# A hybrid decoder trunk on Trainium2: weight halves between the RWKV triangular products one place further ahead, the fourth gate chunk in two halves, one merge behind the masks

## What is computed

```python
z = x @ w_in[l]
z_s5, z_lx, z_ly, z_rw, z_gate = jnp.split(z, IN_SPLITS, axis=-1)
y_s5 = s5_branch(z_s5, ...)      # ends with (y @ glu_w1) * sigmoid(y @ glu_w2)
y_lru = rglru_branch(z_lx, z_ly, ...)
y_rw = rwkv7_branch(z_rw, ...)   # per token: state = state*w + (state@a) b^T + v k^T
gates = jax.nn.sigmoid(z_gate.reshape(bsz, seq, N_BRANCH, D_MODEL))
merged = gates[:, :, 0] * y_s5 + gates[:, :, 1] * y_lru + gates[:, :, 2] * y_rw
x = layer_norm(ALPHA * x + merged @ mix_w_out[l], ln2_g[l], ln2_b[l])
```

## Time and profile before

| | before |
|---|---|
| median of 3 runs | 1610.47 us (1610.46 to 1610.76) |
| the profiled execution | 1610.43 us, span 1608.4 us |
| TensorE matmul busy | 1576.7 us, 98% of the span |
| VectorE busy | 1254.2 us, 78% |
| ScalarE busy | 796.2 us, 50% |
| granted TensorE clock | full (0.998 on the mean) |

### The profile page before, as it was taken

One profiled execution on the slowest core, in us unless ns is written; L12 is line 12 of the kernel. 1 busy time (PEld: TensorE's weight loads), 2 busy tenths in 40 slices (PEclk: granted clock), 3 DMA queues, 4 the chain that ended last, 5 costly groups with the idle time before them and its releaser, 6 DMA issues. The chain is left out here.

```text
span 1608.4 us, 31364 instructions
## 1 busy us (share of the span) xinstructions
PE 1576.7 (98%) x13277; PEld 1417.2 (88%) x13277; DVE 1254.2 (78%) x1620; ACT 796.2 (50%) x1018; POOL 234.2 (15%) x167
## 2 busy tenths in 40 slices
PE   9999999999999999999999999999999999999997
PEld 8888889999989988888888888999999999888886
DVE  6799899798668858766688998998885678587666
ACT  4655453663454545444455555346543545454443
POOL 2024520000000302001110435100000003010101
PEclk9999999999999999999999999999999999999999
DMA  8765744433436545666776656554334465456663
GB/s 250 216 190 183 207 135 136 138 121 107 147 118 210 171 130 171 186 193 186 210 199 188 191 177 182 158 145 125 113 117 145 128 210 165 144 163 191 190 190 131
DMA packets 380915, 267.74 MB, mean 166 GB/s; under 512 B 21132, under 2 KB 361576, under 8 KB 380776
## 3 DMA queue, kind: packets, MB, share of 16 engines
q1 hardware_dynamic: 377548, 255.16, 53.4%
q10 hardware_dynamic: 3228, 10.58, 2.1%
HBM read 264.66 MB, written 1.05 MB: 165 GB/s over the span
## 5 line engine op out<-in xcount | busy, mean ns | idle before, releaser
L1812 DVE TENSOR_TENSOR ring_lo<-ring_raw,ring_hi 128x1024 fp32r<-128x1024 f32 x461 | 598.0, 1302 | 200.4 <-ACT ring_hi L1389 195.8
L1389 ACT ACTIVATE ring_hi<-ring_raw 128x1024 fp32r<-128x1024 f32 x472 | 497.8, 1057 | 459.8 <-PE bank L765 203.2
L762 PE MATMUL bank<-xT,ring_hi 128*128 128x512 f32 x1344 | 335.5, 391 | 0.0
L762 PEld LDWEIGHTS bank<-xT,ring_hi 128*128 128x128 f32 x1344 | 244.1, 189 | 45.5
L735 PE MATMUL bank<-xT,ring_hi 128*128 128x256 f32 x864 | 251.3, 291 | 4.1 <-DVE ring_lo L1812 3.6
L736 PE MATMUL bank<-xT,ring_hi 128*128 128x256 f32 x864 | 244.3, 283 | 0.0
L737 PE MATMUL bank<-xT,ring_lo 128*128 128x256 f32 x864 | 244.2, 283 | 0.0
L765 PEld LDWEIGHTS bank<-xT,ring_lo 128*128 128x128 f32 x1344 | 183.3, 190 | 13.2 <-DVE ring_lo L1812 0.2
L765 PE MATMUL bank<-xT,ring_lo 128*128 128x256 f32 x1344 | 187.5, 282 | 0.0
L735 PEld LDWEIGHTS bank<-xT,ring_hi 128*128 128x128 f32 x864 | 165.3, 191 | 10.4 <-issue 5.4
L736 PEld LDWEIGHTS bank<-xT,ring_hi 128*128 128x128 f32 x864 | 165.5, 192 | 0.6 <-issue 0.5
(11 more groups left out here) (349 smaller groups left out, 2533.3 us busy)
## 6 DMA issues: line engine op xcount, KB each, us to landing
ring_raw<-in_w_in_dram SPq DMA_DIRECT2D x100, 512.0 KB, 4.0
ring_raw<-in_ffn_wg_dram SPq DMA_DIRECT2D x88, 512.0 KB, 3.9
ring_raw<-in_ffn_wu_dram SPq DMA_DIRECT2D x88, 512.0 KB, 3.9
ring_raw<-in_ffn_wd_dram SPq DMA_DIRECT2D x88, 512.0 KB, 3.4
ring_raw<-in_xa_wkv_dram SPq DMA_DIRECT2D x32, 512.0 KB, 3.9
ring_raw<-in_s_glu_w_dram SPq DMA_DIRECT2D x16, 512.0 KB, 3.4
ring_raw<-in_mix_w_out_dram SPq DMA_DIRECT2D x16, 512.0 KB, 3.9
ring_raw<-in_xa_wq_dram SPq DMA_DIRECT2D x16, 512.0 KB, 4.2
```

The lines of the kernel that those rows point to most:

```text
L762: mm(both, hi[:, k, :], xT_both[:, :, k, :], start=(k == 0), stop=(k == ND - 1), skip_group_check=True)
L1389: return nc.scalar.activation(o, i, func, **kw)
L1812: st.mark(tt(lo_flat(n), raw_flat(n), hi_flat(i), ALU.subtract), s_lo["dve"])
```

## The change

On TensorE, the three pieces between the four sets of products stand one place earlier: w2 (1,0) ahead of N1 instead of behind it, w2 (1,1) ahead of N2, and the first half of gate (4) ahead of N3. The second half of gate (4) stays behind N3. On VectorE, the low half of w2 (1,1) stands ahead of the V masks, that of gate (4,0) ahead of the M masks, that of gate (4,1) ahead of M plus eye, and `merge(3)` stands behind V plus eye instead of ahead of the W masks. ScalarE, GpSimd and SyncE keep their order. Lines of VectorE are one higher after the change, and some two.

```diff
--- before.py
+++ after.py
@@ -1124,12 +1124,13 @@
                     r = slice(C * par, C * par + C)
                     return mm(o, BK[r, q // NC, q % NC, 0, :], AR[r, q // NC, q % NC, 0, :], start=True, stop=True)
 
+                half_chunk("w2", 1, 0, zu_r)
                 pe.wait_ge(*at(s_Ge, 6))
                 for q in range(0, NQ, 2):
                     for par, qp in ((0, 0), (1, 1), (0, 1), (1, 0)):
                         last = turned_product(par, q + qp, banks[4 + par][C * qp:C * qp + C, q // 2 * C:q // 2 * C + C])
                 last.then_inc(s_N, 1)
-                half_chunk("w2", 1, 0, zu_r)
+                half_chunk("w2", 1, 1, zu_r)
                 pe.wait_ge(*at(s_Ge, 8))
                 pe.wait_ge(*at(s_Nb, 2))
                 for q in range(NQ):
@@ -1138,7 +1139,7 @@
                                                                                  (q % 8) * C:(q % 8 + 1) * C])
                         if q == NQ - 1:
                             last.then_inc(s_N, 1)
-                half_chunk("w2", 1, 1, zu_r)
+                half_chunk("gate", 4, 0, xT)
                 pe.wait_ge(*at(s_Nb, 4))
                 for q in range(NQ):
                     for par in range(2):
@@ -1147,7 +1148,7 @@
                                   AR[r, q // NC, q % NC, 0, :], BK[r, q // NC, q % NC, 0, :], start=True, stop=True)
                         if q == NQ - 1:
                             last.then_inc(s_N, 1)
-                gate(4)
+                half_chunk("gate", 4, 1, xT)
 
                 fill = [("gate", 5, xT), ("gate", 6, xT), ("gate", 7, xT), ("lru", 0, ly_r), ("lru", 1, ly_r)]
                 ORDER = ((0, 0), (1, 1), (0, 1), (1, 0))
@@ -2322,6 +2323,7 @@
                 st.then(stt(th_, h_, 1.0, th_, ALU.add, ALU.mult), s_lq)
                 masked_G(2)
                 masked_G(3)
+                lo_to("w2", 1, further=False)
 
                 def lru(t):
                     st.then(v.tensor_tensor_scan(h_[:, t, :], a_[:, t, :], gi_[:, t, :], 0.0, ALU.mult, ALU.add))
@@ -2337,16 +2339,14 @@
                 for par in range(2):
                     st.mark(tt(V_[:, par], bank(4 + par, 8, C),
                                const("off1T").unsqueeze(1).to_broadcast([P, NQ // 2, C]), ALU.mult), s_Nb)
-                lo_to("w2", 1, further=False)
                 merge(2)
+                lo_to("gate", 4, 0, further=False)
                 for par in range(2):
                     dve.wait_ge(*at(s_N, 2 + par))
                     st.mark(tt(M_[C * par:C * par + C], *masked("strictT", par), ALU.mult), s_Nb)
-                lo_to("gate", 4, 0, further=False)
+                lo_to("gate", 4, further=False)
                 dve.wait_ge(*at(s_Nb, 4))
                 st.mark(tt(M_, M_, eye, ALU.add), s_Me)
-                lo_to("gate", 4, further=False)
-                merge(3)
                 for par in range(2):
                     dve.wait_ge(*at(s_N, 4 + par))
                     st.mark(tt(W_[C * par:C * par + C], *masked("off1", par), ALU.mult), s_Nb)
@@ -2355,6 +2355,7 @@
                 lo_to("gate", 5, 0, further=False)
                 V16 = V_.rearrange("p a k c -> p (a k) c")
                 st.then(tt(V16, V16, eye, ALU.add), s_Vi)
+                merge(3)
                 dve.wait_ge(*at(s_lm, 1))
                 st.then(tt(gi_, gi_, th_, ALU.mult))
```

## The result

The median went from 1610.47 to **1617.44 us** (five executions each, 1616.65 to 1618.66 after). The ratio is 1.0042, with a 95% interval of 1.0032 to 1.0053. The forecast was slower, 1614.3 us, so the direction came as predicted, but 3.84 us were forecast and 7.0 came, and the time lies outside the range of 1612.7 to 1615.3. Further down, one execution of run 5 (1709.28 us at a mean clock of 0.849) and one of run 9 (7006.98 us) stand far from all others, and the ratios leave them out.

A forecast was written before the change was run, and what follows sets the result against it. TensorE, 98% busy at full clock, was taken as the bound; W products 1.92 us later in each of two layers gave 3.84 us on 1610.43, so 1614.3 us. The 8-in-10 range was 1612.7 to 1615.3.

The forecast's parts named there:

- What bounds the kernel: Whole kernel: TensorE is busy 98% of the span at full clock, so only its few gaps can pay.
- TensorE's side: TensorE from the last G products to Y: earlier halves remove the wait before N1, 0.57 us per layer at most.
- the 0.57: TensorE's idle us before the first N product, waiting for a mask of G; only 0.08 was forecast to reach Y.
- VectorE's side: VectorE up to Y: about 1.1 us new stall before the M masks; W masks start at 373.94 after N3.
- Behind Y: Gate (5,0) waits for merge (3)'s bank: about 2.7 us idle on TensorE, W products 1.92 us later per layer.
- The next round: Behind the W product: VectorE has more room than before, so the shift stays 1.92 us and nothing is added.
- 2 x 1.92 = 3.84 us: Total over two layers of the later W products, added to the profiled 1610.43 us to give 1614.3.
- the fourth rival: Clock falls to 1.2 GHz behind the new gap before gate (5,0): at most 6.1 us more, 1620.4 us; 5%.
- The sentence on the Trainium skill: It says idle time returns the array's clock to half rate, making a clock fall likelier; countered by "the trace shows no fall".
- The first: The bank doesn't decide; VectorE's late Y masks start the W product 1.3 us later than now: 1613.1 us; 10%.
- The second: Small TensorE gaps further behind shrink by 0.8 us per layer, giving part of the delay back: 1612.7 us; 8%.
- The third: Merge (3) ends before 379.0, so this stretch's four gaps close, gaining 1.75 us per layer: 1607.0 us; 3%.

The follow-up runs named there:

- run 5: Changed kernel with merge (3) ahead of the M masks instead of behind V plus eye; 1610.78 us, ratio 0.9999.
- run 9: Kernel before the change with only the gating of the LRU input moved behind the Y masks of round 0; 1610.52 us, ratio 0.9998.
- run 8: Changed kernel with merge (3) one place earlier, behind the low half of gate (5,0) and ahead of V plus eye; 1614.88 us, ratio 1.0022.
- run 1: Changed kernel with merge (3) back ahead of the W masks, the rest of the change kept; 1613.68 us, ratio 1.0018.
- run 3: Changed kernel with 20 unread transposes between the Y products of round 0 and gate (5,0); 1614.87 us, ratio 1.0025.
- run 7: Changed kernel with 6 unread transposes in the idle 0.85 us before the Y products; 1617.16 us, ratio 1.0041.
- run 10: Changed kernel with merge (3) ahead of V plus eye and 11 unread transposes in the idle time before gate (5,0); 1613.69 us, ratio 1.0018.
- run 12: Changed kernel with merge (3) back ahead of the W masks and 16 unread transposes in the idle time before Y; 1613.23 us, ratio 1.0016.
- run 2: Kernel before the change with only merge (3) moved behind V plus eye; 1612.10 us, ratio 1.0008.
- run 11: Changed kernel with 10 unread transposes right behind the Y products, filling part of the idle time before gate (5,0); 1614.46 us, ratio 1.0023.
- run 4: Changed kernel with the gating of the LRU input behind the Y masks of round 0 instead of ahead; 1616.94 us, ratio 1.0037.

## Why the prediction was wrong

**What bounds the kernel, and TensorE's side.** Right. Every start up to Y came within 0.03 us of the sum, and 0.08 us of the 0.57 arrived.

**VectorE's side.** Right. The new stall before the M masks is 1.17 us (forecast 1.1), and the W masks are tied to N3: they start at 373.94 as forecast.

**Behind Y.** Right: gate (5,0) waited 2.59 us (forecast "about 2.7 us") for merge (3), and for nothing else: with that merge one place further ahead the wait is 1.45 (run 8), and ahead of the masks there is none (runs 1 and 5). Run 3 prices the wait at 4.05 us in all against 3.84. The next round held, too.

**The step that failed** is the sum, "2 x 1.92 = 3.84 us": it kept every product at full clock behind the new gap. The clock was the fourth rival, with 5%, argued down with "the granted clock stayed full through every gap of the trace, 2.75 us at the very start included". That row did not bear the argument: 2.75 us before the first product of the program is not a gap between products, and the longest gap inside the program in those rows is 0.57 us (0.9 in the whole trace). There was no row of before for 2.6 us of idle time in the midst of work, and so no reason for a chance as low as 5%.

The trace of before even had three signs of the other side. First, right behind those 2.75 us the products are slow: the ten records of L949 in the earlier trace rows take 2.34 us to the next row (5.09), 0.23 each, and the same product takes 0.12 a little later:

```profile
8.08 2.17 PE L959 MATMUL bank<-constants 128*128 128x128 f32 x18
```

That is the factor between the two levels of the clock, although the profile's column gives 1.00 for both; which of the two misleads was not tried. Second, the granted clock does fall at the end of the program, where TensorE's last product is over at 1598.36. That idle time is longer than the 2.7 us in question, but the fall is in the trace, and the page's row of 9s doesn't show it:

```profile
1600.00:1602.00 2.00, 0.00 (x0) 0.00 (x0) 1.93 (x4) 0.00 (x0) 1.05 (x1) 0.90 0.00 0
1602.00:1604.00 2.00, 0.00 (x0) 0.00 (x0) 1.97 (x2) 0.00 (x0) 0.41 (x1) 0.50 0.00 0
```

A slice of that row is 40 us long, so a fall as short as the ones here still rounds to 9. Third, the kernel before fills some of its own waits with the transposes of runs 3 and 7, by a helper whose name says what for, `keep_clocked` (L892): eleven of them stand from 611.19 on, ahead of products that start at 613.13.

The rival's price was a bound, "at most" 3.06 us per layer; it measured 1.47 and 1.45, half of it. In the first layer the clock was still full for the first 1.5 us of gate (5,0) and recovered during the W products; in the second it was down from the start but back before the half chunk was over. With that size the fourth rival would have given 1614.3 + 2.9 = 1617.2, against 1617.44 measured.

The sentence on the Trainium skill, "TensorE: Matmul & The Clock Gate", Part 1, named the right case: idle time brings the array back to half rate, and here the trace agrees, with 0.50 between 384 and 386. It was weighed and set aside with "the trace shows no fall", which the rows above contradict.

**The other rivals.** The first (VectorE's lateness alone) lies 0.5 us behind the bank's wait, as forecast, and shows as soon as the bank is out of the way and the clock is kept: run 10 has 0.71 us of idle time there. The second (given back later) did not come: run 3 kept all of the wait to the end. The third, the other side, did not come; run 5, with merge (3) covered, reached 1610.78 and not 1607.0, because the gaps before Y and W are VectorE's chain from N3 on, which covering merge (3) doesn't shorten.

## What to carry to other kernels

Where TensorE is the bound, an instruction on another engine that releases a PSUM bank belongs ahead of the last place where TensorE can do without that bank; look in the list of waits for the count that it raises, not only for its result. VectorE's newly idle stretch is the place for it: the same merge there cost nothing. And price a new gap of TensorE twice, once for the wait and once for the products behind it at half clock, unless the trace has a gap as long in the midst of work; a few products that nobody reads are a cheap way to tell the two apart. To see whether a clock fell, read windows of 2 us and how long like products take; slices of 40 us hide it.

## What the runs showed of the hardware

The clock fell between dense stretches after less idle time than I had thought. By idle time of TensorE around the Y products, one layer:

| run | idle before Y | work between | idle before gate (5,0) | clock behind it |
|---|---|---|---|---|
| 3 | 0.84 | 3.5 | 0.25 | full in 9 of 9 |
| 12 | 0.36 | | none | full in 11 of 11 |
| 10 | 0.84 | 2.5 | none | full in 11 of 11 |
| 2 | 0 | | 1.71 | full in at least 10 of 11 |
| 11 | 0.85 | 2.4 | 1.35 | full in 11 of 11 |
| 1 | 2.11 | | none | fell in some |
| 8 | 0.85 | 1.16 | 1.45 | fell in some |
| 7 | 0.19 | 1.16 | 2.59 | fell in 5 of 5 |
| 4 | 0.85 | 1.16 | 2.59 | fell in at least 4 of 5 |
| after | 0.85 | 1.16 | 2.59 | fell in 5 of 5 |

"Full" and "fell" are read from the mean clock of each execution (0.998 against 0.996, with 0.997 between) and its time; only the profiled executions show the place. The 0.002 that is missing even in a full one is the end of the program, where TensorE has nothing left to do and the clock is at 0.50 for nearly 7 us. A fall cost 1.47 and 1.45 us in the two layers after the change, and between 1.3 and 1.5 in the profiles of runs 4 and 7 (by their way from the last G products to the Y products of round 1, against run 3). In run 8 it cost 0.6 to 0.7, since there the W products would have waited 0.71 us for the masked Y anyway (run 10). In the first layer it set in not at once but 1.5 us after the work began again. In the second layer it had already set in: the first product there (1182.33) takes 0.58 us instead of 0.39. By the windows of runs 4, 7 and 8 it came between 0.4 us ahead of the first product and 1.3 us behind it, so the place varies. Why runs 1 and 8 differ from one execution to the next with the same program was not tried.
